# Bias and score matmuls moved between the key transposes of a chunk, the bias of two chunks issued as a pair, in the sample attention of a hybrid decoder step

## What is computed

```python
kp = cache_k[page_table].reshape(DB, past, H, Dh)          # DB 8, past 2048, H 8, Dh 64
vp = cache_v[page_table].reshape(DB, past, H, Dh)
suffix = (lax.cumsum(lfp, axis=1, reverse=True) - lfp).transpose(0, 2, 1)
s_past = jnp.einsum('bqhd,bkhd->bhqk', q, kp).astype(jnp.float32) * scale
s_past = s_past + suffix[:, :, None, :] + cn[:, :, :, None]
s_new  = jnp.einsum('bqhd,bkhd->bhqk', q, k).astype(jnp.float32) * scale
...
p = jax.nn.softmax(jnp.concatenate([s_past, s_new], axis=-1), axis=-1)
o = (jnp.einsum('bhqk,bkhd->bqhd', p[..., :past].astype(v.dtype), vp)
     + jnp.einsum('bhqk,bkhd->bqhd', p[..., past:].astype(v.dtype), v))
```

## Time and profile before

| | us |
|---|---|
| median of 3 runs (2093.55 to 2097.01) | 2096.53 |
| the profiled execution's own time | 2094.77 |
| its span, from first to last instruction | 2093.1 |
| TensorE busy over the span | 1942.8 |
| sample attention, first matmul of `own_scores` to the next stage's first matmul | 786.28 to 1008.83 |

### The profile page before, as it was taken

How to read it: one execution, slowest core, us unless ns; L and a number is a source line. 1 busy time by engine, 2 the same in 40 slices (tenths; PEclk the granted TensorE clock), 3 DMA queues, 4 the chain that set the end, 5 groups by cost and what they waited for, 6 DMA issues and landing times. The chain is left out here.

```text
span 2093.1 us, 23171 instructions
## 1 busy us (share of the span) xinstructions
PE 1942.8 (93%) x8461; PEld 1029.7 (49%) x8461; DVE 602.4 (29%) x1405; ACT 302.9 (14%) x500; POOL 186.8 (9%) x290
## 2 busy tenths in 40 slices
PE   8999998799999988898899998789999999994897
PEld 4465444556566655555555555344444444441443
DVE  4201113423334333444232223311111111110686
ACT  1000001112223222333110001300000000000110
POOL 1000003200000002333000000100000000000220
PEclk9988999899999999999899998989999999997899
DMA  7120100261111227998521243469999999995341
GB/s 256 15 81 3 44 21 0 65 255 66 46 66 46 67 81 269 332 326 318 211 75 52 75 172 128 155 254 407 415 421 422 425 418 423 421 423 198 124 140 51
DMA packets 108816, 406.25 MB, mean 194 GB/s; under 512 B 18825, under 2 KB 36298, under 8 KB 96354
## 3 DMA queue, kind: packets, MB, share of 16 engines
q1 hardware_dynamic: 85138, 331.27, 41.2%
q0 software_dynamic: 16496, 56.15, 7.4%
q10 hardware_dynamic: 7072, 17.38, 2.1%
HBM read 354.48 MB, written 50.27 MB: 193 GB/s over the span
## 5 line engine op out<-in xcount | busy, mean ns | idle before, releaser
L1986 PE MATMUL psum<-arena 128*64 128x512 f32 (+1 forms) x1024 | 344.0, 599 | 1.4 <-DVE arena L2076 1.4
L802 PE MATMUL psum<-arena 128*128 128x363 f32 (+1 forms) x768 | 255.1, 477 | 10.1 <-DMA arena<-in_w_in 8.4
L1986 PEld LDWEIGHTS psum<-arena 128*64 128x64 f32 (+1 forms) x1024 | 130.1, 165 | 181.1 <-issue 179.3
L287 PE MATMUL psum<-arena 128*128 128x512 f32 x432 | 190.1, 600 | 0.0
L802 PEld LDWEIGHTS psum<-arena 128*128 128x128 f32 x768 | 140.2, 192 | 84.4 <-DMA arena<-in_w_in 8.6
L2023 PE MATMUL psum<-arena 128*64 128x512 f32 (+1 forms) x512 | 170.0, 595 | 1.0 <-DVE arena L2090 1.0
L287 PEld LDWEIGHTS psum<-arena 128*128 128x128 f32 x432 | 82.6, 193 | 100.3 <-issue 100.3
L2327 PE MATMUL psum<-arena 128*128 128x512 f32 x288 | 127.8, 602 | 1.4 <-DVE arena L2357 1.4
L1466 PE MATMUL psum<-arena 128*128 128x512 f32 x288 | 125.7, 594 | 1.6 <-PEq L1323 1.6
L2023 PEld LDWEIGHTS psum<-arena 128*64 128x64 f32 (+1 forms) x512 | 66.1, 163 | 101.9 <-issue 101.9
L2076 DVE TENSOR_TENSOR arena<-psum,g_moe_rows 128x1024 f32<-128x1024 f32 x24 | 29.4, 1224 | 276.4 <-PE psum L1980 276.4
(11 more groups left out here) (267 smaller groups left out, 1943.2 us busy)
## 6 DMA issues: line engine op xcount, KB each, us to landing
arena<-in_w_exp_gate SPq DMA_DIRECT2D x32, 2048.0 KB, 14.0
arena<-in_w_exp_up SPq DMA_DIRECT2D x32, 2048.0 KB, 14.6
arena<-in_w_exp_down SPq DMA_DIRECT2D x32, 2048.0 KB, 11.0
arena<-in_cache_k SPq DMA_DIRECT2D x128, 256.0 KB, 4.7
arena<-in_cache_v POOLq DMA_DIRECT2D x128, 256.0 KB, 5.7
moe_out<-arena ACTq DMA_DIRECT2D x24, 512.0 KB, 11.9
arena<-in_w_in SPq DMA_DIRECT2D x5, 2048.0 KB, 19.9
moe_out<-arena SPq DMA_DIRECT2D x1, 9728.0 KB, 32.0
```

Source lines behind the costliest of these rows:

```text
L287: last = mm(c.bank[4 + r % 3][:, :], HT[:, k, t * P:(t + 1) * P], W[:, n + 1, k, :], start=(k == 0), stop=(k == KD - 1))
L802: done = mm(c.bank[7][:, 0:b - a], WG[:, blk % 2, k, q * P:(q + 1) * P], HT[:, k, a:b], start=(k == 0), stop=(k == KD - 1))
L1986: last = mm(out[rows_, :], XT[:, u % 2, k, rows_], c.ring_tile(LOAD[kind, u, r])[:, k, :], start=(k == 0), stop=(k == KD - 1))
```

## The change

TensorE's order is written anew. A chunk `n` is now T0, then (odd chunks only) the biases of chunks n-1 and n one right behind the other, T1, T2, the scores of chunk n-1, and T3. The bias of even chunks takes `SPREAD` and `SUF` from partitions 0 to 7 and that of odd chunks from partitions 64 to 71, so `SUF` is loaded in four pieces of 8x512 in place of one of 8x2048, and `SPREAD` is built twice. The pair waits for `page_biased` of the chunk before it (both banks must be free), the scores no longer do. The last chunk's bias, which stood behind the last-but-one sequence's `weigh`, is now issued ahead of it.

```diff
--- before.py
+++ after.py
@@ -966,8 +966,13 @@
     VC = view(c, W_AT, NCH, CH, WA)
     KTS = view(c, Q_AT, 2, NPAIR, CH * P)
     S = view(c, K_AT, 2, PAST)
-    SUF = view(c, V_AT, 2, PAST)[0:H]
-    SPREAD = view(c, HT_AT + 2 * WBLK, P)[0:H]
+    SUF = view(c, V_AT, 2, PAST)
+    SPREAD = view(c, HT_AT + 2 * WBLK, P)
+
+    def bias_rows(ch):
+
+        return slice(64 * (ch % 2), 64 * (ch % 2) + H)
+
     NONE = view(c, HT_AT + 2 * WBLK + P, CH * P)
     t0 = T_AT
     QB = view(c, t0, 2, NPAIR * STRIP)
@@ -1005,7 +1010,9 @@
             for b in range(DB):
                 if b >= 2:
                     sp.wait_ge(chunk_mm, NCH * (b - 1))
-                sp.dma_start(SUF[:, b % 2, :], c.sufd[:, b, :]).then_inc(bias_in[b % 2], 16)
+                for ch in range(NCH):
+                    keys = slice(ch * 512, ch * 512 + 512)
+                    sp.dma_start(SUF[bias_rows(ch), b % 2, keys], c.sufd[:, b, keys]).then_inc(bias_in[b % 2], 16)
                 if b == 0:
                     continue
                 for ch in range(NCH):
@@ -1034,33 +1041,52 @@
         def _(pe):
             mm, tp = nc.tensor.matmul, nc.tensor.transpose
 
-            def turn_keys(b, ch):
-                pe.wait_ge(k_in[ch], 64 * (b + 1))
-                for j in range(NPAIR):
-                    u = U * b + NPAIR * ch + j
-                    if u >= 2:
-                        pe.wait_ge(kt_a if j % 2 else kt_v, u // 2)
-                    for g in range(CH):
-                        last = tp(c.bank[2 + j % 2][:, g * P:(g + 1) * P], KC[:, ch, g, j * P:(j + 1) * P], c.ident[:])
-                    last.then_inc(k_tr, 1)
+            def turn_keys(n, j):
+
+                b, ch = n // NCH, n % NCH
+                u = NPAIR * n + j
+                if j == 0:
+                    pe.wait_ge(k_in[ch], 64 * (b + 1))
+                if u >= 2:
+                    pe.wait_ge(kt_a if j % 2 else kt_v, u // 2)
+                for g in range(CH):
+                    last = tp(c.bank[2 + j % 2][:, g * P:(g + 1) * P], KC[:, ch, g, j * P:(j + 1) * P], c.ident[:])
+                last.then_inc(k_tr, 1)
+
+            def two_biases(n):
+
+                b = n // NCH
+                if n == 0:
+                    pe.wait_ge(blanked, 6)
+                if n % NCH == 0:
+                    pe.wait_ge(bias_in[b % 2], 64 * (b // 2 + 1))
+                if n >= 1:
+                    pe.wait_ge(ttr, n)
+                for m in (n, n + 1):
+                    ch = m % NCH
+                    mm(c.bank[ch % 2][:, :], SPREAD[bias_rows(ch)], SUF[bias_rows(ch), b % 2, ch * 512:(ch + 1) * 512],
+                       start=True, stop=False, skip_group_check=True)
 
             def scores(n):
 
                 b, ch = n // NCH, n % NCH
                 pe.wait_ge(kt_v, 2 * (n + 1))
                 pe.wait_ge(kt_a, 2 * (n + 1))
-                if n >= 2:
-                    pe.wait_ge(ttr, n - 1)
-                if n == 0:
-                    pe.wait_ge(blanked, 4)
-                if ch == 0:
-                    pe.wait_ge(bias_in[b % 2], 16 * (b // 2 + 1))
-                mm(c.bank[ch % 2][:, :], SPREAD, SUF[:, b % 2, ch * 512:(ch + 1) * 512],
-                   start=True, stop=False, skip_group_check=True)
                 for j in range(NPAIR):
                     last = mm(c.bank[ch % 2][strip(j), :], QB[:, b % 2, strip(j)], KTS[:, ch % 2, j, :], start=False,
                               stop=True, skip_group_check=True)
                 last.then_inc(chunk_mm, 1)
+
+            def next_keys(n):
+
+                turn_keys(n, 0)
+                if n % 2 == 1:
+                    two_biases(n - 1)
+                turn_keys(n, 1)
+                turn_keys(n, 2)
+                if n >= 1:
+                    scores(n - 1)
+                turn_keys(n, 3)
 
             def own_scores(b):
                 pe.wait_ge(qb_done, 2 * b + 2)
@@ -1115,20 +1141,15 @@
 
             for b in range(DB):
                 own_scores(b)
-                turn_keys(b, 0)
-                if b >= 1:
-                    scores(NCH * b - 1)
-                turn_keys(b, 1)
-                scores(NCH * b)
+                next_keys(NCH * b)
+                next_keys(NCH * b + 1)
                 if b >= 2:
                     turn_out(b - 2)
-                turn_keys(b, 2)
-                scores(NCH * b + 1)
+                next_keys(NCH * b + 2)
                 if b >= 1:
                     turn_weights(b - 1, 0)
                     turn_weights(b - 1, 1)
-                turn_keys(b, 3)
-                scores(NCH * b + 2)
+                next_keys(NCH * b + 3)
                 if b >= 1:
                     turn_weights(b - 1, 2)
                     turn_weights(b - 1, 3)
@@ -1266,10 +1287,12 @@
             v.memset(NONE, 0.0).then_inc(blanked, 1)
             v.memset(SPREAD, 0.0).then_inc(blanked, 1)
             dve.wait_ge(blanked, 2)
-            cells = SPREAD.rearrange("h (j s) -> h j s", s=STRIP)
-            for half in range(2):
-                v.tensor_copy(cells[:, :, half * DT:(half + 1) * DT], bcast(c.ident[0:H, half:H:2], DT)
-                              ).then_inc(blanked, 1)
+            for ch in range(2):
+                r = bias_rows(ch)
+                cells = SPREAD[r].rearrange("h (j s) -> h j s", s=STRIP)
+                for half in range(2):
+                    v.tensor_copy(cells[:, :, half * DT:(half + 1) * DT],
+                                  bcast(c.ident[r, r.start + half:r.stop:2], DT)).then_inc(blanked, 1)
             dve.wait_ge(zeroed, 3)
             dve.wait_ge(cn_in, 16 * H)
             spread(0)
```

## The result

The changed kernel took 2070.22 us (median of 4 runs, 2068.32 to 2073.61), the kernel before 2095.04 us in the 4 runs on the same chip (2093.36 to 2097.01). The ratio is 0.9883 with an interval of 0.9865 to 0.9901: 1.2% faster, clear of the noise. It is faster by more than I predicted: 2070.22 lies some 7 us under the forecast and 0.8 us under the range's low end of 2071. In a second comparison, with more runs of both, the changed kernel took 2073.77 us (6 runs) and the kernel before 2093.43 us (24 runs), ratio 0.990 (0.9879 to 0.9922): a gain of 19.7 us.

A forecast was written before the change was run, and what follows sets the result against it. TensorE was taken to set the pace, DMA close behind. Pairs 12.5 us and waits bring 21.8 us, less 2.5 for DMA, plus 0.5 for clock: 19.8 us off 2094.77, plus 1.76 to the median, forecast 2077 us, range 2071 to 2087.5.

The forecast's parts named there:

- price of a pair: Two biases in different row groups on TensorE overlap and cost 1.06 us together; bounds 1.06 to about 1.95 us.
- waits a period: TensorE's waits in front of key transposes fall from 3.27 to 1.62 us a period: 0.51 in chunk 0, 1.1 in chunk 2.
- period: TensorE's repeating period in the sample attention falls from 25.74 to 22.2 us through two pairs and shorter waits.
- start to K chunk 5: At the sample attention's start, time saved on TensorE only lengthens its wait for K chunk 5: 0 us gained.
- gain from K chunk 5 to `weigh` of sequence 6: From 812.31 to 984.06 us, pairs give 12.5 us and shorter waits the rest, together 21.8 us.
- charge for DMA lag: DMA can't fully follow the shorter periods: 0 to 8 us over six periods, charged at 2.5 us.
- clock: With fewer waits TensorE's clock may not fall in part of one period: at most 1.6 us, taken as 0.5.
- the end: The closing chain through GpSimd and DMA for the last V pages, 19.6 us, stays as it is.
- the stage: Net gain in the sample attention: 21.8 - 2.5 + 0.5 = 19.8 us.
- DMA takes over: Rival: 365 GB/s in every period (23.5 us) and a slower tail leave a gain of 10 to 15 us; chance 0.15.
- the last step, from the gain to the time: Whole kernel: 19.8 us off the profiled 2094.77, plus 1.76 us up to the median, gives 2076.8 us.
- every rival inside the stage: In the sample attention: DMA binds (0.15), pair doesn't overlap (0.10), better overlap (0.08), pair held up by VectorE, slower (0.03).

The follow-up runs named there:

- experiment 2: Changed kernel with both biases of a pair taken from partitions 0 to 7, one row group: 2083.72 us, ratio 0.9957 to the kernel before.
- experiment 4: Changed kernel with ScalarE's exponentials behind chunk 0's copies and the first two weight-transpose groups between T0 and T1 of chunk 2: 2077.07 us, ratio 0.9936.
- experiment 5: Only 256 of 512 columns of each V page loaded: in the changed kernel 2049.43 us, in the kernel of experiment 4 2057.34 us.
- experiment 7: Kernel of experiment 4 with sequence 0's V pages also held back until the transposes of chunks 0 to 2 are done: 2067.96 us, ratio 0.9883.

## Why the prediction was right, and where it missed

| step of the prediction | forecast | measured |
|---|---|---|
| price of a pair | 1.06 us | 1.06 us; 1.91 us with both in one row group |
| pair waits for both banks | 0 | 0, by 0.18 us |
| waits a period | 1.62 us | 1.46 us |
| period | 22.2 us | 22.03 us |
| start to K chunk 5 | no gain | 26.11 against 26.03 us, no gain |
| gain from K chunk 5 to `weigh` of sequence 6 | 21.8 us | 171.75 - 149.92 = 21.83 us, in part by cancellation |
| charge for DMA lag | 2.5 us | none there |
| clock | +0.5 us | +0.58 us in periods 2 to 6; behind the K wait some 1.9 us lost |
| the end | as it is | 25.97 against 24.77 us, 1.2 us lost |
| the stage | 19.8 us | 20.55 us |
| everything outside the stage | as it is | 5.10 us less ahead of it, 0.13 more behind it |

**The mechanism held.** The overlap of two contractions of 8 was the largest unknown, and the earlier trace rows priced it right. The Trainium skill, "TensorE: Matmul & The Clock Gate", Part 3, has this concurrency for contractions of 32 in different row groups; this case shows it for 8, and experiment 2 shows that the row groups are what does it. The waits went where the steps put them, with one difference: in chunk 2 I had 1.1 us in front of T3, and 0.57 us of it stands one group earlier, in front of T2, for VectorE. The sum is the same within 0.2 us, since a T3 that comes later waits less.

**The 21.8 us are in part luck.** By the starts of `own_scores` the forecast has 0.9 us from K chunk 5 to sequence 2, 17.9 in the five periods of sequences 2 to 6, and 3.0 from sequence 7 to `weigh` of sequence 6. Measured are -0.4, 19.1 and 3.2. In the first stretch the changed kernel lost to the clock what it had won: behind the 4.60 us wait T0, pair, T1, T2 and scores took 6.56 us (807.29 to 813.85) for work priced at 3.63, where the kernel before lost 1.0 us behind its wait of 2.90. The periods gave more, 3.71 us each in place of 3.58, and one of them ran for less time at the lower clock (22.52 us for a period of 22.03, where 26.80 stood for 25.73).

**The DMA charge was in the wrong place.** I charged 2.5 us for lags that gather over the middle periods. None did: a period moves 32 pages of 256 KB and 64 KB of suffix, 8.45 MB, which at 22.03 us is 384 GB/s, and that is what the windows show, 380. At the end 1.2 us were lost, and hardly to DMA: the waits for V are 0.29, 1.63 and 1.49 us in place of 0.33 and 1.51, but the chain to the last of them is only 0.22 us longer, for TensorE comes to the waits earlier (the bias of chunk 31 is gone from this stretch); the other 0.98 us are the lower clock behind the two waits. "DMA takes over" did not come at 22 us. Experiments 4, 5 and 7 show that it comes at 21: a period of 20.97 us would need 8.45 / 20.97 = 403 GB/s, and the most that a window of a middle period showed is 384. The Trainium skill, "DMA: Bandwidth & Descriptors", section Specifications, puts the HBM limit of a core at about 358 GB/s, which is a stack's 716 divided by its two cores. Here one core was at work, and 380 to 384 were sustained, so that share is no cap for it. Taken as a cap, it would have put the period at 23.6 us or more, by estimate from 8.45 MB, and 22.03 were measured.

**What failed is the last step, from the gain to the time:** "The profiled execution would take 2094.77 - 19.8 = 2075.0 us; the median of the runs is 1.76 us above it, so 2076.8, put at 2077 us". This step takes the time outside the stage over as it is, a term of zero for which I gave no reason. It measured 5.10 us ahead of the stage, 4.04 of them in the gated MLP, with TensorE's clock at 0.98 where it was 0.92. Of the 6.6 us between 2076.8 and 2070.22 that is the largest part; the stage adds 0.75, and the median of the four runs lay 0.97 us above the profiled run in place of 1.76. The gain itself is sized well: 20.55 us in the stage between the first profiles (up to 24.18 between others), and 19.7 us between the medians of the long comparison. The base is high too: the median of three runs lay 3 to 5 us above those of 24 and 13 runs. My range held every rival inside the stage and nothing for this. With 19.8 us taken off 2093.43 the forecast would have been 2073.6, beside 2073.77 measured in the same comparison; in the first comparison, with its four runs each, 2095.04 - 19.8 would still be 5 us above 2070.22. That the 5 us are chance and no effect of the change is shown as far as the second run of the changed kernel lacks most of them (785.14) and kernels of every kind, the one before too, lie on both sides; what puts the MLP stage at 96 us in one execution and at 99 to 100 in another stays open.

## What to carry to other kernels

Small contractions that leave most rows of the array unused can go in pairs in different row groups and banks, for the price of one, if what must free both banks has been done; here that alone took 2.07 us off a period and 13 us off the median. What a matmul at one place saves can uncover a wait at another: here the exponentials in chunk 2. Price such a change in the order in which its covers vanish: whoever shortens the work between two copies should look for the copy that is queued behind something long, on another engine. And before giving a range, look at how much the unchanged part of the kernel moves between runs: here medians of the same kernel differed by up to 5 us and the start of the stage by 8, more than any single term of the sum was off. A wait for a load also costs more than its length when the clock falls behind it: look at the rows that follow it.

## What was not expected of the hardware

- Behind every K wait of 2.85 us or more in these traces TensorE came back at 1.2 GHz, the lower of its two levels. In the changed kernel, behind 4.60 us, the pair took 2.01 us (810.34 - 808.33) in place of 1.06, and the window's clock is 0.85; behind 3.45 us in experiment 4 it was the same. So such a wait costs more than its length, here 2.9 and 4.1 us. Nor does a shorter one always go free: behind the 1.85 us in experiment 5 the pair took 1.67 us. Behind the 1.09 us at 799.01 the next eight transposes took their usual 1.09 us. Of the two short waits at the end, the one of 1.63 us left 32 matmuls at 1.08 us, and with the one of 1.49 us behind it they took 1.68.
- DMA held a share of 1.04 and 380 GB/s over whole periods with two queues, one of SyncE and one of GpSimd, both with pages of 256 KB, without TensorE noticing.
